# Stage A of a hybrid attention and MoE step: a round's work on ScalarE and VectorE reordered, the weight copy cut in two, the second adaLN half moved

## The chip, the cores and the metric

The kernel runs on one core of a Trainium2 chip. The metric is the device time of one execution in microseconds. A core has TensorE (matmul), VectorE, ScalarE, GpSimd and SyncE (which here only issues DMAs); each runs its own instruction stream in order, and they meet at semaphores. In rows of the profile they are PE (and PEld for the load of its weights), DVE, ACT, POOL and SP.

## The reference, cut to what matters

One layer for 256 prompt rows and 64 sample rows of width 1024, float32:

```python
h = RMSNorm(x) * (1 + scale1) + shift1          # scale, shift: adaLN, mod = silu(c) @ w_ada + b_ada
proj = h @ w_in                                 # A: q|k|v, B: q|k|v, gate_A, gate_B
# A: 8 heads, two 64-wide softmax maps per head (q, k RMS-normed, rotary), values 128 wide
s = einsum(q, k); p = softmax(where(mask, s, NEG_INF))
a = p[0] - lam * p[1]
o = rmsnorm(a @ v, subln_g) * (1 - lam_init)
# B: stick-breaking attention, 16 heads of 64
mix = sigmoid(gate_A) * (A @ w_oa) + sigmoid(gate_B) * (B @ w_ob)
x += gate1 * (mix @ w_out)
x += gate2 * HierMoE(RMSNorm(x) * (1 + scale2) + shift2)   # top-2 of 8 experts in 1 of 4 groups
```

The change is in stage A: the projection of the A columns and the differential attention. All its quantities are still computed.

## The kernel before

The stages follow each other: norm and first adaLN columns, stage A (to about 241 us), the gate and output product of A, stage B, its mix, the output product, the router and the experts.

Stage A is a software pipeline over the 8 heads. The function `a_iteration(h, ...)` exists once on each of the engines TensorE, ScalarE and VectorE; it is called for h = 0 to 10 (h = 4 to 7 from a hardware loop), and each call is what the text calls a round. Round h works on four heads at once:

- it projects head h (`P_on`, h up to 7): first the 64 sample rows as one float32 product (`proj_sample`, 32 matmuls), then tile 0 and tile 1 of 128 prompt rows each (`proj_tile`), each of 8 steps of 3 matmuls, since a float32 product is made of high and low parts: hi x hi, hi x lo, lo x hi (`mm3`, L546 to L548);
- it norms, rotates and transposes q and k of head h-1 (`qk_on`, h = 1 to 8) and makes the scores and exponentials of its prompt part (the first part of its maps);
- it makes the sample part of the maps of head h-2 and the transposes of the finished map (`s1_on`, h = 2 to 9);
- it makes the product with the values (PV), the norm and the transposes of the output of head h-3 (`o_on`, h = 3 to 10), and with it two chunks of the later adaLN columns (`ada_chunk(h, 0)` and `ada_chunk(h, 1)`, 32 small matmuls each, into bank 1, columns 384 to 511).

TensorE's order in a steady round: sample projection; PV; ada_chunk 0; scores of the sample part; tile 0; transposes of `o_n` (L688); four transposes of q and k (L696); ada_chunk 1; a wait for `a_olo`, that is for VectorE's `oT_lo`, which reads the bank that the next transposes write; four more transposes (L701); tile 1; transposes of the map (L716); scores of the prompt part.

ScalarE's order: `sq` (squares of q and k, L1093); root for q and k (`ss_ln`, `rs`: L1036, L1038); the whole high part of the next head's weights `w_hi` (`split`, L1069); copy of the sample's projection to `stage` (`stage_out(2, 0)`, L1111); `osq` (squares of PV, L1121) and root `o_rs`; exponentials of the sample part (L1127); copy of tile 0 (L1115); `oT_hi` (L1134); copy of half of the q/k transposes (L1138); copy of tile 1; `late_rows` (the adaLN results, L1143); copy of the map's transposes `aT` (L1146); exponentials of the prompt part (L1151).

VectorE's order: `ss` (sums of `sq`, L1433); q and k times `rs` ("scale", L1437); `o_ss` (sums of `osq`, L1441); `o_n` (L1445); maximum of the sample part (L1449) and its negation `a_nmx` (L1451); `combine` (L1417 to L1425: the two maps into `amap`); `oT_lo` (L1457); copy of the other half of the q/k transposes (L1461); the low part of the weights `w_lo` (L1365); rest of `aT` (L1466); maxima and combine of the prompt part.

GpSimd multiplies q and k by their gains (L1754), rotates them (L1764 to L1768, the last one gives `a_roped`) and keeps the values (L1773). SyncE issues, in a round and in this order: the next weights (`a_weights`, after `split_done` and the sample's projection), four stores of `stage` (`a_store`, after `a_roped`), the caches, and the two adaLN chunks (`load_late`, each after a chunk was used, by `late_used`). A copy to `stage[j]` waits until the stores of two heads before have landed (`a_stored[j]`). Weights and staging have double buffers (`raw`, `w_hi`, `w_lo`, `stage`). The next sample projection waits for `split_done`, which VectorE's `w_lo` gives.

Of the kernel before, what the change touches and what calls it, by code (L numbers as in the profile page):

```python
# [7 lines left out]
P = 128  # L8
D = 1024
# [70 lines left out]
def build(nc, t_in, t_out):  # L80
    g = t_in
    ctx = ExitStack()
    with ctx:
        def sem(name):
            return ctx.enter_context(nc.semaphore(name))
# [65 lines left out]
        sq = take("sq", [P, TILES, 256])  # L151
        osq = place("osq", [P, TILES, P], F32, cursor[0] - 4 * TILES * 256)
        ss = take("ss", [P, 12])
# [10 lines left out]
        a_sum = take("a_sum", [P, 2, 3])  # L164
        a_rec = take("a_rec", [P, 2, 3])
        o_ss = take("o_ss", [P, 3])
        o_ln = take("o_ln", [P, 3])
        o_rs = take("o_rs", [P, 3])
        o_n = take("o_n", [P, TILES, P])
        h_sample = take("h_sample", [P, KD, DEC])  # L170
        a_end = cursor[0]
# [5 lines left out]
        assert ada_at[4] + 8 * D + 2 * D <= raw_at  # L177
        late_rows = place("late_rows", [P, D], F32, hT_at - 4 * KD * PADDED)
        ada_late = [take(f"ada_late{n}", [P, KD, ADA_COLS]) for n in range(2)]
# [106 lines left out]
        h_mod = sem("h_mod"); h_hi = sem("h_hi"); h_ready = sem("h_ready")  # L286
        split_hi = sem("split_hi"); split_done = sem("split_done");

# [51 lines left out]
        def f32(ap):  # L340
            return ap.bitcast(F32)
# [198 lines left out]
        def _(pe):  # L540
# [108 lines left out]
            def a_iteration(h, j, P_on, qk_on, s1_on, o_on, cache_value):  # L649
# [34 lines left out]
                if o_on:  # L684
                    l = h - 3
                    pe.wait_ge(a_on, l + 1)
                    for t in range(TILES):
                        last = nc.tensor.transpose(ps[:, 4, t * P:(t + 1) * P], o_n[:, t, :], ident)  # L688
                    last.then_inc(a_oT, 1)
                if qk_on:  # L690
                    m = h - 1
                    pe.wait_ge(a_roped, m + 1)
                    pe.wait_ge(a_cache[jq], cache_value)
                    st = stage[jq]
                    for n, src in enumerate((st[:, 0, 0:P], st[:, 1, 0:P], st[:, 2, 0:P], st[:, 0, P:2 * P])):
                        nc.tensor.transpose(ps[:, 3, n * P:(n + 1) * P], src, ident)  # L696
                    if o_on:
                        ada_chunk(h, 1)
                        pe.wait_ge(a_olo, h - 2)
                    for n, src in enumerate((st[:, 1, P:2 * P], a_kc[jq][:, 0, :], a_kc[jq][:, 1, :], st[:, 2, P:2 * P])):  # L700
                        last = nc.tensor.transpose(ps[:, 4, n * P:(n + 1) * P], src, ident)  # L701
                    last.then_inc(a_qkT, 1)
                elif o_on:
                    ada_chunk(h, 1)
                if P_on:
# [32 lines left out]
            for n in range(8):  # L738
                last = nc.tensor.transpose(ps[:, 5 + n // 4, (n % 4) * P:(n % 4 + 1) * P], late_rows[:, n * P:(n + 1) * P], ident)
            last.then_inc(col_T, 1)  # L740
# [281 lines left out]
        def _(act):  # L1022
# [38 lines left out]
            def split(j, loaded, used, width=UNIT):  # L1061
# [7 lines left out]
                A(w_hi[j][:, :, 0:width], raw[j][:, :, 0:width], ACT.Copy).then_inc(split_hi, 1)  # L1069

            split(0, None, None)
            act.wait_ge(ada_used, KD)
# [3 lines left out]
            for t in range(2):  # L1076
                for half in range(2):
                    ks = slice(4 * half, 4 * half + 4)
                    act.wait_ge(h_mod, 2 * t + half + 2)
                    A(hT_hi[:, ks, t * P:(t + 1) * P], h_full[:, ks, t * P:(t + 1) * P], ACT.Copy).then_inc(h_hi, 1)  # L1080
            A(hT_hi[:, :, SEQ:TOK], h_sample[:], ACT.Copy).then_inc(h_hi, 1)
            act.wait_ge(lam_dve, 1)
            A(lam_exp[:], lam_sum[:], ACT.Exp).then_inc(lam_act, 1)

            def a_iteration(h, j, P_on, qk_on, s1_on, o_on, loaded, store_value):
                jq = 1 - j
                if qk_on:
                    act.wait_ge(a_staged, 3 * h)
                    if isinstance(h, int) and h == 1:
                        act.wait_ge(setup_done, 2)  # L1090
                    else:
                        act.wait_ge(a_ss, h - 1)
                    A(sq[:], stage[jq][:, :, 0:256], ACT.Square).then_inc(a_sq, 1)  # L1093
                    act.wait_ge(a_ss, h)
                    if not (isinstance(h, int) and h == 1):
                        act.wait_ge(a_scaled, h - 1)
                    root(rs[:], ss_ln[:], ss[:], 64, a_rs)
                if loaded is not None:
                    split(jq, loaded, None if isinstance(h, int) and h == 0 else (a_proj, 3 * h),
                          MIX_COLS if isinstance(h, int) and h >= 7 else UNIT)  # L1100

                def stage_out(t, n):
# [11 lines left out]
                    else:  # L1114
                        A(stage[j][:, t, :], ps[:, t, 0:UNIT], ACT.Copy).then_inc(a_staged, 1)  # L1115

                if P_on:
                    stage_out(2, 0)
                if o_on:
                    act.wait_ge(a_pv, h - 2)  # L1120
                    A(osq[:], ps[:, 7, 0:PADDED].rearrange("p (t c) -> p t c", t=TILES), ACT.Square).then_inc(a_osq, 1)  # L1121
                    act.wait_ge(a_oss, h - 2)
                    root(o_rs[:], o_ln[:], o_ss[:], P, a_ors)
# [8 lines left out]
                if o_on:  # L1132
                    act.wait_ge(a_oT, h - 2)
                    A(oT_hi[:, bass.ds(h - 3, 1), :].rearrange("p a n -> p (a n)"), ps[:, 4, 0:TOK], ACT.Copy,  # L1134
                      scale=subln[:, 0:1]).then_inc(a_ohi, 1)
                if qk_on:
                    act.wait_ge(a_qkT, h)
                    A(qkT[:, 0:512], ps[:, 3, :], ACT.Copy).then_inc(a_qkT_act, 1)  # L1138
                if P_on:
                    stage_out(1, 2)  # L1140
                if o_on:
                    act.wait_ge(late_used, 2 * h - 4)
                    A(late_rows[:, bass.ds((h - 3) * P, P)], ps[:, ADA_BANK, 384:512], ACT.Copy).then_inc(late_out, 1)  # L1143
                if s1_on:
# [165 lines left out]
        def _(dve):  # L1310
# [89 lines left out]
            dve.wait_ge(h_hi, 5)  # L1400
            V.tensor_tensor(hT_lo[:, :, SEQ:TOK], h_sample[:], f32(hT_hi[:, :, SEQ:TOK]), ALU.subtract).then_inc(h_ready, 1)
            dve.wait_ge(rows_in, 144)
# [26 lines left out]
            def a_iteration(h, j, qk_on, s1_on, o_on, split_on):  # L1429
                jq = 1 - j  # L1430
                if qk_on:
                    dve.wait_ge(a_sq, h)
                    V.tensor_reduce(ss[:].rearrange("p (t n) -> p t n", t=TILES),  # L1433
                                    sq[:].rearrange("p t (n c) -> p t n c", n=4), AX, ALU.add).then_inc(a_ss, 1)
                    dve.wait_ge(a_rs, h)
                    st = stage[jq][:, :, 0:256].rearrange("p t (n c) -> p t n c", n=4)
                    V.tensor_tensor(st, st, rs[:].rearrange("p (t n) -> p t n", t=TILES).unsqueeze(3).broadcast_to([P, TILES, 4, 64]),  # L1437
                                    ALU.mult).then_inc(a_scaled, 1)
                if o_on:
                    dve.wait_ge(a_osq, h - 2)  # L1440
                    V.tensor_reduce(o_ss[:], osq[:], AX, ALU.add).then_inc(a_oss, 1)  # L1441
                    dve.wait_ge(a_ors, h - 2)
# [19 lines left out]
                if split_on:  # L1462
                    split(h + 1, jq, MIX_COLS if isinstance(h, int) and h >= 7 else UNIT)
                if s1_on:
# [456 lines left out]
```

## Time and profile before

| | |
|---|---|
| median of 3 runs | 859.41 us (856.08 to 861.2) |
| profiled execution, its own time | 860.19 us |
| its span in the profile | 858.5 us |
| TensorE matmul busy | 714.1 us (83%) |
| VectorE busy | 347.3 us (40%) |
| ScalarE busy | 270.1 us (31%) |
| GpSimd busy | 102.1 us (12%) |
| mean granted clock of TensorE | 0.933 of full speed |

The span counts from the first to the last instruction. Matmuls are pipelined: their ends are modelled and overlap the next one's start, so a busy TensorE isn't one at its peak. A number in square brackets behind a row is the idle time of that engine before it, with the instruction that ended it. An engine that isn't the bottleneck may be idle without costing anything.

### The profile page before, as it was taken

The numbers are of one execution on the slowest core, as the hardware profiler recorded it, in microseconds if no ns is written. First come the engines' busy times: TensorE is split into PE (matmuls) and PEld (weight loads), VectorE is DVE, ScalarE is ACT, GpSimd is POOL, SyncE is SP. The second block draws the span as 40 slices with busy tenths as digits, with TensorE's granted clock in tenths as the row PEclk, the third lists the DMA queues.
The fourth block names the chain that finished last, engine by engine and source line by source line (L and its number), as shares of the span: only waits on it lengthen the run. The fifth ranks groups of instructions, "written<-read, shape, count | busy, mean of one in ns | idle before, by whom it ended". The sixth has DMA issues, their size and how long they took to land.

```text
span 858.5 us, 13770 instructions
## 1 busy us (share of the span) xinstructions
PE 714.1 (83%) x5329; PEld 586.5 (68%) x5329; DVE 347.3 (40%) x539; ACT 270.1 (31%) x490; POOL 102.1 (12%) x161
## 2 busy tenths in 40 slices
PE   0798888899799799999988999736998888788770
PEld 0487777788599798999987999634654554545440
DVE  0656555556534334333442356541233113213225
ACT  1454455454335254444544442300111011101100
POOL 2011111111000001010010000010011100100014
PEclk9899999999899899999999999857999999999985
DMA  9966466555643666452315443499899999999805
GB/s 323 321 167 197 132 181 176 174 172 175 195 152 111 175 172 226 118 139 63 110 44 163 147 133 113 165 424 416 324 418 417 418 418 418 417 417 419 332 17 183
DMA packets 131176, 199.17 MB, mean 232 GB/s; under 512 B 11688, under 2 KB 113464, under 8 KB 117816
## 3 DMA queue, kind: packets, MB, share of 16 engines
q1 hardware_dynamic: 123032, 185.63, 61.1%
q0 software_dynamic: 6208, 11.02, 3.6%
q10 hardware_dynamic: 1888, 1.86, 0.7%
q8 instruction: 32, 0.52, 0.2%
q14 instruction: 16, 0.13, 0.0%
HBM read 193.47 MB, written 16.55 MB: 245 GB/s over the span
## 4 chain that ended last, share of the span: by engine, by line
PE 52%; issue 22%; ACT 9%; DVE 8%; DVEq 3%; POOL 2%; POOLq 2%; ACTq 1%; DMA 0%
PE ps L551 29%; PE ps L546 6%; PE ps L548 6%; PE ps L547 6%; ACT w_hi L1069 3%; DVE w_lo L1365 2%; ACT probs L1151 1%; PE ps L948 1%; PE ps L952 1%; PE ps L984 1%; ACT probs L1127 1%; DVE amap L1425 1%; DVEq L1450 1%; PE ps L716 1%; DVE ss L1433 1%
## 5 line engine op out<-in xcount | busy, mean ns | idle before, releaser
L551 PE MATMUL ps<-e_w,xgT 128*64 128x256 f32 x1024 | 130.2, 418 | 31.9 <-issue 30.7
L551 PEld LDWEIGHTS ps<-e_w,xgT 128*64 128x64 f32 x1024 | 91.8, 151 | 66.1 <-issue 37.4
L1365 DVE TENSOR_TENSOR w_lo<-raw,w_hi 128x2048 fp32r<-128x2048 f32 (+1 forms) x36 | 100.5, 2793 | 86.2 <-ACT w_hi L1069 86.2
L546 PE MATMUL ps<-hT_hi,w_hi 128*128 128x320 f32 x320 | 102.7, 321 | 5.5 <-DVE w_lo L1365 5.2
L548 PE MATMUL ps<-hT_hi,w_lo 128*128 128x320 f32 x320 | 100.0, 312 | 0.0
L547 PE MATMUL ps<-hT_lo,w_hi 128*128 128x320 f32 x320 | 99.9, 312 | 0.0
L1069 ACT ACTIVATE w_hi<-raw 128x2048 fp32r<-128x2048 f32 (+1 forms) x36 | 83.2, 2310 | 28.5 <-PE ps L548 28.5
L1686 DVE TENSOR_SCALAR h_s<-h_e 128x256 f32<-128x256 f32 x16 | 4.7, 294 | 162.3 <-ACT h_e L1282 162.3
L546 PEld LDWEIGHTS ps<-hT_hi,w_hi 128*128 128x128 f32 x320 | 61.2, 191 | 7.9 <-DVE w_lo L1365 5.5
L547 PEld LDWEIGHTS ps<-hT_lo,w_hi 128*128 128x128 f32 x320 | 61.2, 191 | 0.0
L548 PEld LDWEIGHTS ps<-hT_hi,w_lo 128*128 128x128 f32 x320 | 61.1, 191 | 0.0
L551 PE MATMUL ps<-e_w,hidT 128*64 128x512 f32 x256 | 58.4, 598 | 0.6 <-ACT hidT L1288 0.6
L1282 ACT ACTIVATE h_e<-ps 128x256 f32<-128x256 f32 x16 | 6.1, 384 | 153.7 <-PE ps L551 153.7
L546 PE MATMUL ps<-w_hi,hT_hi 128*128 128x384 f32 x128 | 44.3, 346 | 0.0
L548 PE MATMUL ps<-w_hi,hT_lo 128*128 128x384 f32 x128 | 42.9, 335 | 0.0
L547 PE MATMUL ps<-w_lo,hT_hi 128*128 128x384 f32 x128 | 42.8, 335 | 0.0
L1860 POOL DMA_INDIRECT expert_rows<-y_sb,idx x16 | 16.2, 1012 | 215.0 <-DVE y_sb L1699 200.8
L546 PE MATMUL ps<-oT_hi,w_hi 128*128 128x320 f32 x128 | 40.4, 315 | 1.1 <-DVE oT_lo L1524 1.1
L547 PE MATMUL ps<-oT_lo,w_hi 128*128 128x320 f32 x128 | 40.3, 315 | 0.0
L548 PE MATMUL ps<-oT_hi,w_lo 128*128 128x320 f32 x128 | 40.2, 314 | 0.0
L551 PEld LDWEIGHTS ps<-e_w,hidT 128*64 128x64 f32 x256 | 17.5, 136 | 29.6 <-issue 27.8
L551 PE MATMUL ps<-ada_late,c_cols 128*32 128x128 f32 x512 | 33.1, 285 | 0.0
(258 smaller groups left out, 1225.6 us busy)
## 6 DMA issues: line engine op xcount, KB each, us to landing
e_w<-in_w SPq DMA_DIRECT2D x96, 1024.0 KB, 18.3
raw<-in_w_in SPq DMA_DIRECT2D x45, 512.0 KB
ada_late<-in_w_ada SPq DMA_DIRECT2D x16, 1024.0 KB, 5.0
ada_first<-in_w_ada SPq DMA_DIRECT2D x8, 1024.0 KB, 21.3
raw<-in_w_in SPq DMA_DIRECT2D x8, 1024.0 KB
raw<-in_w_oa SPq DMA_DIRECT2D x4, 1024.0 KB
raw<-in_w_ob SPq DMA_DIRECT2D x4, 1024.0 KB
raw<-in_w_out SPq DMA_DIRECT2D x4, 1024.0 KB
```

The costliest lines, as they stand in the source:

```text
L546: nc.tensor.matmul(out, lhs_hi, rhs_hi, start=first, stop=False, skip_group_check=True)
L547: nc.tensor.matmul(out, lhs_hi, rhs_lo, start=False, stop=False, skip_group_check=True)
L548: return nc.tensor.matmul(out, lhs_lo, rhs_hi, start=False, stop=last, skip_group_check=True)
L551: return nc.tensor.matmul(out, lhs, rhs, start=first, stop=last, skip_group_check=True)
L716: last = nc.tensor.transpose(ps[:, b, c * P:(c + 1) * P], amap[:, n * P:(n + 1) * P], ident)
L948: last = nc.tensor.transpose(ps[:, 0, k * P:(k + 1) * P], xg[p % RING][:, k:D:KD], ident)
L952: last = nc.tensor.transpose(ps[:, 1, (k - 4) * P:(k - 3) * P], xg[p % RING][:, k:D:KD], ident)
L984: last = nc.tensor.transpose(ps[:, 4, m * P:(m + 1) * P], hid[j][:, m:FE:2], ident)
L1069: A(w_hi[j][:, :, 0:width], raw[j][:, :, 0:width], ACT.Copy).then_inc(split_hi, 1)
L1127: last = A(probs[mp][:, 384:704], ps[:, 5 + mp, 0:320], ACT.Exp, bias=a_nmx[:, mp, 2:3], accum_out=a_sum[:, mp, 2:3])
L1365: V.tensor_tensor(w_lo[j][:, :, 0:width], raw[j][:, :, 0:width], f32(w_hi[j][:, :, 0:width]), ALU.subtract).then_inc(split_done, 1)
L1860: G.indirect_dma_start(y_dram, bass.IndirectOffsetOnAxis(ap=idx[:, 1, p:p + 1], axis=0), y_sb[j][:], None, bounds_check=2 * TOK, oob_is_er ...
```

## The change

On ScalarE a round now runs: sq; copy of the sample's projection; osq; root for q and k; root `o_rs`; exponentials; copy of tile 0; oT_hi; the first half of the weights' high part (the first 4 of 8 row blocks); its half of the q/k copy; the second half; the rest as before. On VectorE `o_ss` stands before the scaling of q and k, and the low part is made in two halves, each after its half of the high part. On TensorE `ada_chunk(h, 1)` stands directly behind the transposes of `o_n`, before those of q and k. `osq` gets memory of its own in place of the tail of `sq`; `h_sample` and `late_rows` move into the columns of `xnT` that are free.

```diff
-        osq = place("osq", [P, TILES, P], F32, cursor[0] - 4 * TILES * 256)
+        osq = take("osq", [P, TILES, P])
-        h_sample = take("h_sample", [P, KD, DEC])
-        late_rows = place("late_rows", [P, D], F32, hT_at - 4 * KD * PADDED)
+        late_rows, h_sample = xnT[:, :, 0:P], xnT[:, :, TOK:PADDED]
@@ TensorE
                     last.then_inc(a_oT, 1)
+                    ada_chunk(h, 1)
                 if qk_on:
...
                     if o_on:
-                        ada_chunk(h, 1)
                         pe.wait_ge(a_olo, h - 2)
...
-                elif o_on:
-                    ada_chunk(h, 1)
@@ ScalarE
+            def split_first(j, loaded, used, width):
+                act.wait_ge(raw_loaded[j], loaded - 48 * (1 - j))
+                if used is not None:
+                    act.wait_ge(*used)
+                A(w_hi[j][:, 0:KD // 2, 0:width], raw[j][:, 0:KD // 2, 0:width], ACT.Copy).then_inc(split_half, 1)
+            def split_second(j, width):
+                A(w_hi[j][:, KD // 2:KD, 0:width], raw[j][:, KD // 2:KD, 0:width], ACT.Copy).then_inc(split_hi, 1)
...
                 if qk_on:
                     act.wait_ge(a_staged, 3 * h)
...
                     A(sq[:], stage[jq][:, :, 0:256], ACT.Square).then_inc(a_sq, 1)
-                    act.wait_ge(a_ss, h)
-                    if not (isinstance(h, int) and h == 1):
-                        act.wait_ge(a_scaled, h - 1)
-                    root(rs[:], ss_ln[:], ss[:], 64, a_rs)
-                if loaded is not None:
-                    split(jq, loaded, None if isinstance(h, int) and h == 0 else (a_proj, 3 * h),
-                          MIX_COLS if isinstance(h, int) and h >= 7 else UNIT)
                 if P_on:
                     stage_out(2, 0)
                 if o_on:
                     act.wait_ge(a_pv, h - 2)
+                    if not (isinstance(h, int) and h == 3):
+                        act.wait_ge(a_oss, h - 3)
                     A(osq[:], ps[:, 7, 0:PADDED].rearrange("p (t c) -> p t c", t=TILES), ACT.Square).then_inc(a_osq, 1)
+                if qk_on:
+                    act.wait_ge(a_ss, h)
+                    if not (isinstance(h, int) and h == 1):
+                        act.wait_ge(a_scaled, h - 1)
+                    root(rs[:], ss_ln[:], ss[:], 64, a_rs)
+                if o_on:
                     act.wait_ge(a_oss, h - 2)
                     root(o_rs[:], o_ln[:], o_ss[:], P, a_ors)
...
+                width = MIX_COLS if isinstance(h, int) and h >= 7 else UNIT
+                if loaded is not None:
+                    split_first(jq, loaded, None if isinstance(h, int) and h == 0 else (a_proj, 3 * h), width)
                 if qk_on:
                     act.wait_ge(a_qkT, h)
                     A(qkT[:, 0:512], ps[:, 3, :], ACT.Copy).then_inc(a_qkT_act, 1)
+                if loaded is not None:
+                    split_second(jq, width)
@@ VectorE
+                if o_on:
+                    dve.wait_ge(a_osq, h - 2)
+                    V.tensor_reduce(o_ss[:], osq[:], AX, ALU.add).then_inc(a_oss, 1)
+                if qk_on:
                     dve.wait_ge(a_rs, h)
...
                 if o_on:
-                    dve.wait_ge(a_osq, h - 2)
-                    V.tensor_reduce(o_ss[:], osq[:], AX, ALU.add).then_inc(a_oss, 1)
                     dve.wait_ge(a_ors, h - 2)
...
                 if split_on:
-                    split(h + 1, jq, MIX_COLS if isinstance(h, int) and h >= 7 else UNIT)
+                    width = MIX_COLS if isinstance(h, int) and h >= 7 else UNIT
+                    for n, (signal, value) in enumerate(((split_half, h + 1), (split_hi, h + 2))):
+                        ks = slice(n * KD // 2, (n + 1) * KD // 2)
+                        dve.wait_ge(signal, value)
+                        last = V.tensor_tensor(w_lo[jq][:, ks, 0:width], raw[jq][:, ks, 0:width], f32(w_hi[jq][:, ks, 0:width]),
+                                               ALU.subtract)
+                    last.then_inc(split_done, 1)
```

## Rows read from the trace of the kernel before

**Rows 1.** Stretches: us, busy us (instructions) of each engine, clock, DMA share, GB/s

```profile
108.60:200.40 91.80, 81.93 (x743) 71.54 (x741) 51.93 (x96) 43.98 (x108) 16.68 (x24) 1.00 0.61 184
320.00:410.00 90.00, 88.87 (x708) 82.30 (x707) 33.50 (x41) 41.18 (x58) 10.10 (x30) 1.00 0.48 141
```

**Rows 2.** Waits of TensorE from 90 to 205: total us, times, longest

```profile
PE ps L701 <- DVE oT_lo L1457: 6.3, 5, 1.5
PE ps L688 <- DVE o_n L1445: 5.8, 5, 1.2
```

**Rows 3.** Timeline of TensorE, round 5: start, us, instruction [idle before]

```profile
131.49 2.82 PE L551 MATMUL ps<-raw,h_sample 128*64 128x192 f32 x32
...
135.77 1.94 PE L551 MATMUL ps<-ada_late,c_cols 128*32 128x128 f32 x32
...
142.48 0.34 PE L548 MATMUL ps<-w_hi,hT_lo 128*128 128x384 f32 x1
143.97 0.55 PE L688 MATMUL ps<-cst,o_n 128*128 128x128 f32 x3 [1.15 <-DVE o_n L1445]
...
144.88 1.94 PE L551 MATMUL ps<-ada_late,c_cols 128*32 128x128 f32 x32
148.33 0.33 PE L701 MATMUL ps<-cst,stage 128*128 128x128 f32 x1 [1.51 <-DVE oT_lo L1457]
...
154.60 2.82 PE L551 MATMUL ps<-raw,h_sample 128*64 128x192 f32 x32
```

**Rows 4.** Timeline of ScalarE, round 5

```profile
134.94 0.85 ACT L1093 ACTIVATE sq<-stage 128x768 f32<-128x768 f32 x1
137.75 0.30 ACT L1036 ACTIVATE ss_ln<-ss,eps 128x12 f32<-128x12 f32 x1 [1.96 <-DVE ss L1433]
...
138.30 2.78 ACT L1069 ACTIVATE w_hi<-raw 128x3072 fp32r<-128x3072 f32 x1
140.97 0.65 ACT L1111 ACTIVATE stage<-ps 64x192 f32<-64x192 f32 x2
```

**Rows 5.** Timeline of VectorE, round 5

```profile
136.77 0.95 DVE L1433 TENSOR_REDUCE ss<-sq 128x12 f32<-128x768 f32 x1
138.37 0.96 DVE L1437 TENSOR_TENSOR stage<-stage,rs 128x768 f32<-128x768 f32 x1 [0.65 <-ACT rs L1038]
...
143.83 0.82 DVE L1449 TENSOR_REDUCE a_mx<-ps 128x2 f32<-128x640 f32 x1
...
147.73 0.55 DVE L1457 SCALAR_TENSOR_TENSOR oT_lo<-ps,subln,oT_hi 128x320 f32 x1
```

**Rows 6.** Groups by form, 60 to 345 us: busy us, mean ns | idle before

```profile
L1365 DVE TENSOR_TENSOR w_lo<-raw,w_hi 128x3072 fp32r<-128x3072 f32 x11 | 36.9, 3352 | 18.1 <-ACT w_hi L1069 18.1
...
L1365 DVE TENSOR_TENSOR w_lo<-raw,w_hi 128x2048 fp32r<-128x2048 f32 x7 | 16.0, 2291 | 24.4 <-ACT w_hi L1069 24.4
```

**Rows 7.** Timelines of round 1: TensorE, ScalarE, GpSimd

```profile
54.18 2.82 PE L551 MATMUL ps<-raw,h_sample 128*64 128x192 f32 x32 [1.35 <-DVE w_lo L1365]
...
61.21 0.60 PE L696 MATMUL ps<-cst,stage 128*128 128x128 f32 x4
...
55.25 0.31 ACT L1036 ACTIVATE ss_ln<-ss,eps 128x12 f32<-128x12 f32 x1 [1.02 <-DVE ss L1433]
...
60.35 0.60 POOL L1768 TENSOR_TENSOR stage<-rope_x,rope_y 128x192 f32<-128x192 f32 x1
```

**Rows 8.** Timeline of TensorE, round 8

```profile
215.41 0.33 PE L701 MATMUL ps<-cst,stage 128*128 128x128 f32 x1 [0.53 <-DVE oT_lo L1457]
```

**Rows 9.** Timelines of round 2: VectorE and GpSimd

```profile
75.88 1.13 DVE L1451 TENSOR_SCALAR a_nmx<-a_mx 128x2 f32<-128x2 f32 x1
...
75.15 1.84 POOL L1754 TENSOR_TENSOR stage<-stage,gqk 128x768 f32<-128x768 f32 x1 [13.75 <-DVE stage L1437]
```

**Rows 10.** Timeline of SyncE's issues; landing times of DMAs of `stage`, 147 to 170

```profile
154.95 0.54 SPq L390 DMA_DIRECT2D out_a_v_sample<-stage  x1
...
DMA to landing us min/median/max: 3.5/4.0/5.5
```

More of the change, by code:

```diff
@@ L286, in build @@
         h_mod = sem("h_mod"); h_hi = sem("h_hi"); h_ready = sem("h_ready")
-        split_hi = sem("split_hi"); split_done = sem("split_done");
+        split_half = sem("split_half"); split_hi = sem("split_hi"); split_done = sem("split_done");
         a_cache = [sem(f"a_cache{j}") for j in range(2)]
@@ L738, in _ @@
             for n in range(8):
-                last = nc.tensor.transpose(ps[:, 5 + n // 4, (n % 4) * P:(n % 4 + 1) * P], late_rows[:, n * P:(n + 1) * P], ident)
+                last = nc.tensor.transpose(ps[:, 5 + n // 4, (n % 4) * P:(n % 4 + 1) * P], late_rows[:, n, :], ident)
             last.then_inc(col_T, 1)
@@ L1080, in _ @@
                     A(hT_hi[:, ks, t * P:(t + 1) * P], h_full[:, ks, t * P:(t + 1) * P], ACT.Copy).then_inc(h_hi, 1)
-            A(hT_hi[:, :, SEQ:TOK], h_sample[:], ACT.Copy).then_inc(h_hi, 1)
+            A(hT_hi[:, :, SEQ:TOK], h_sample, ACT.Copy).then_inc(h_hi, 1)
             act.wait_ge(lam_dve, 1)
@@ L1086, in a_iteration @@
                 jq = 1 - j
[L1087 to L1093, printed above, removed]
-                    act.wait_ge(a_ss, h)
-                    if not (isinstance(h, int) and h == 1):
-                        act.wait_ge(a_scaled, h - 1)
-                    root(rs[:], ss_ln[:], ss[:], 64, a_rs)
-                if loaded is not None:
-                    split(jq, loaded, None if isinstance(h, int) and h == 0 else (a_proj, 3 * h),
-                          MIX_COLS if isinstance(h, int) and h >= 7 else UNIT)
                 def stage_out(t, n):
@@ L1115, in stage_out @@
                         A(stage[j][:, t, :], ps[:, t, 0:UNIT], ACT.Copy).then_inc(a_staged, 1)
+                if qk_on:
+                    act.wait_ge(a_staged, 3 * h)
+                    if isinstance(h, int) and h == 1:
+                        act.wait_ge(setup_done, 2)
+                    else:
+                        act.wait_ge(a_ss, h - 1)
+                    A(sq[:], stage[jq][:, :, 0:256], ACT.Square).then_inc(a_sq, 1)
                 if P_on:
@@ L1142, in a_iteration @@
                     act.wait_ge(late_used, 2 * h - 4)
-                    A(late_rows[:, bass.ds((h - 3) * P, P)], ps[:, ADA_BANK, 384:512], ACT.Copy).then_inc(late_out, 1)
+                    A(late_rows[:, bass.ds(h - 3, 1), :].rearrange("p a n -> p (a n)"), ps[:, ADA_BANK, 384:512], ACT.Copy).then_inc(late_out, 1)
                 if s1_on:
@@ L1400, in _ @@
             dve.wait_ge(h_hi, 5)
-            V.tensor_tensor(hT_lo[:, :, SEQ:TOK], h_sample[:], f32(hT_hi[:, :, SEQ:TOK]), ALU.subtract).then_inc(h_ready, 1)
+            V.tensor_tensor(hT_lo[:, :, SEQ:TOK], h_sample, f32(hT_hi[:, :, SEQ:TOK]), ALU.subtract).then_inc(h_ready, 1)
             dve.wait_ge(rows_in, 144)
@@ L1434, in a_iteration @@
                                     sq[:].rearrange("p t (n c) -> p t n c", n=4), AX, ALU.add).then_inc(a_ss, 1)
+                if o_on:
+                    dve.wait_ge(a_osq, h - 2)
+                    V.tensor_reduce(o_ss[:], osq[:], AX, ALU.add).then_inc(a_oss, 1)
+                if qk_on:
                     dve.wait_ge(a_rs, h)
```

## The prediction

> **What bounds the kernel now.** I began with the page's busy shares: TensorE has by far the most work. Then the busy time by stretches, to see the stage that the diff touches [rows 1]: in the steady rounds of stage A TensorE is busy 81.93 of 91.80 us at a granted clock of 1.00, VectorE and ScalarE hardly half, the DMA engines 0.61. Then the waits of TensorE in that stretch, which ask what it lacked [rows 2]: only two things hold it there, 5 times each, once in each of the rounds h = 3 to 7: the transposes of o_n (L688) wait for VectorE's o_n, 5.8 us in all, and the second half of the q/k transposes (L701) waits for VectorE's oT_lo, 6.3 us. So TensorE sets the pace and is held by a chain through ScalarE and VectorE that is late by 1.2 us at two places of a round. Last the timelines of one round on each engine, to see why that chain is late.
>
> I give times in a round as t from the start of its sample projection. Round 5 runs from 131.49 to 154.60, 23.11 us, the first adaLN chunk follows PV at t = 4.3, and tile 0's last matmul starts at 142.48, t = 11.0 [rows 3]. The 24 matmuls of a tile go 0.17 apart, so TensorE could go on at 11.2; the matmul is drawn 0.34 long, so a stop costs the idle time shown (1.15 here) and 0.16 of lost overlap, 0.07 behind the short chunk matmuls. Without its two waits this round is 23.11 - 1.15 - 1.51 - 0.23 = 20.2 us [rows 3]. ScalarE's order is what makes o_n late [rows 4]: sq at 3.45 (to 4.3), the root for q/k at 6.26 when VectorE's ss is there, then the whole weight copy w_hi, 2.78 us, and only at 9.48 the copy of the sample's projection, which TensorE had finished at 2.75, and behind it osq, though PV was ready at 4.3. osq, o_ss, o_n, the map's maximum, exponentials, combine and oT_lo all hang behind this one copy.
>
> **What the change does to a steady round.** ScalarE: sq to 4.3, the sample's copy (0.65) to 4.95, osq (0.5) to 5.45. VectorE is no help earlier: it ends the combine of the former map at 5.3 and ss at 5.28 + 0.94 = 6.2 [rows 5]; o_ss follows to 6.75. The root of ss is not delayed (it waits for ss at 6.26 as before), scale starts at 6.88 as before and ends at 7.84; o_rs is there at 7.4, so o_n runs 7.8 to 8.4. Before, o_n was ready at 12.5. TensorE wants it at 11.2: the first wait is gone, with 2.8 us to spare.
> The map's maximum starts at 8.26 instead of 12.34 (143.83); from its start to oT_lo's end it took 147.73 + 0.55 - 143.83 = 4.45 us [rows 5]. That gives 12.7, with oT_hi ready before it (the transposes of o_n end at 11.7, ScalarE's copy at 12.3). Now the second adaLN half (ada_chunk(h, 1)) stands straight behind the o_n transposes: TensorE comes to L701 at 11.2 + 0.9 for seven transposes (143.97 to 144.88) + 1.9 for the chunk = 14.0 [rows 3]. oT_lo is there 1.3 us before. GpSimd's rope ends 5.7 us after the root starts (60.95 - 55.25 in round 1, rows below), so at 12.0, and is wanted at 13.5. So both waits go. Their worth: 5.8 + 6.3 idle + 5 x (0.16 + 0.07) of lost overlap = 13.3 us over the five rounds.
> The weight halves: VectorE's subtraction costs 2.29 us for 2048 and 3.35 for 3072 elements [rows 6], 1.04 ns each and 0.17 fixed, so two halves cost 0.17 more, ScalarE's likewise about 0.18. In a steady round they lie under the projection of tile 1, 4.2 us: ScalarE's first half 12.3 to 13.8, q/k copy 14.7 to 15.3, second half to 16.7; VectorE's 15.3 to 18.7, the aT copy is wanted at 19.5. Cost nothing; if the cover were gone, 0.2 a round. What is late next: nothing on TensorE, if these sums hold. The move of ada_chunk is 32 matmuls from behind L696 to before it, same work; its data is asked for 18 us ahead. It moves SP's raw and store issues too: they follow late_used, now at t = 13.5.
> Buffers (osq on its own, h_sample and late_rows inside xnT): same instructions, I take zero; nothing of them is on a path with less than 1 us of slack.
>
> **The ends of the loop.** Round 0: the weight copy no longer stands before the copies of the projection, but behind tile 0's, 49.0 to 51.8; VectorE's halves end at 53.8 against 54.13: gain 0.3.
> Round 1 loses. There the root for q/k ran at 55.25, at once, and the rope ended at 60.95, just before TensorE wanted it at 61.21 [rows 7]. In the new order the root is queued behind the copy of the sample's projection, and that is only ready when TensorE ends it: 54.18 + 2.82 - 0.3 = 56.7, and copied by 57.4. The root moves from 55.25 to 57.4, 2.15 later, and scale and rope with it: rope's end 60.95 + 2.15 = 63.1. L696 goes from 61.2 to 63.1: loss 1.9 net of the 0.3. In round 2 the sample is done long before sq, so its root is not moved; its own wait for the rope stays, and nothing there gives the 1.9 back.
> Round 8 (no projection; the gate is TensorE's filler): the wait of 0.53 before L701 [rows 8] and 0.07 overlap go; but there the split stands before the aT copy that TensorE waits for next, and its halves cost 0.1 more: gain 0.5. Rounds 9 and 10 run the same chain as before.
> **Sum:** 13.3 - 1.9 + 0.5 = 11.9 us. All later stages start from it and their loads are gated by the same semaphores, so it goes through to the end. The profiled execution took 860.19 us (span 858.5); that gives 848.3. It lies 0.8 above the median of 859.41, from which the forecast is **847.5**.
>
> **Two contentions.** First, GpSimd. In round 2 VectorE's tiny negation L1451 took 1.13 us instead of 0.17 and ended at 77.01, when GpSimd's L1754, running since 75.15, ended at 76.99 [rows 9]. In the steady rounds of before the rope ran while VectorE was idle. Now L1754 runs from 7.9 to 9.8, over the negation at 9.15: that ends at 9.8, 0.5 later, and the four short rope instructions (to 12) lie over the combine. Bounds: nothing more, or one of them waited for at each of combine's three steps, together 0.9. oT_lo at 13.2 to 14.1 against 14.0; I take 13.3, as in round 2 the combine was hardly longer: no loss. The Trainium skill, "SBUF — State Buffer", section "Who interferes with whom", states that a VectorE instruction in a 2-port mode or with two SBUF inputs and a GpSimd one exclude each other for a whole instruction; the trace agrees with it at L1451, and by it the high bound is the likelier one, 13.3 + 0.7, at the edge.
> Second, the stores. The last store of a round is issued at 154.95, and the stores there take 3.5 to 5.5 us to land [rows 10]; with 3.5 that is 158.45, 13.6 after the second chunk's start at 144.88. Now that start is t = 11.6, so landing is at 25.2, t = 5.0 of the next 20.2-us round, while the sample's copy, which overwrites that stage buffer, could start at 4.3. Before, it started at 9.5 and the landing was hidden. ScalarE will wait 0.7 us here, with osq and both roots behind it; that much goes under ss. Both contentions together put oT_lo at 13.4 to 14.3: low bound no loss, high bound 0.3 a round, 1.5 us.
>
> **Rivals.** (a) The forecast, waits gone and nothing in their place: chance 0.62, own range 845 to 850. It could be some us better: a stretch at half clock follows the waits of rounds 9 and 10, and may fall otherwise.
> (b) oT_lo stays the last to come: the port exclusion at every step, and stores 2 us later than in the trace. Then 1.0 to 1.5 of a round's 2.65 come back: 5 x 1.25 = 6.3, time 853.8. For it: the burst of loads and stores fills the DMA engines already. Against: only sums of bad bounds reach it. It is a slower wait at the same L701. Chance 0.23.
> (c) No change that can be measured (within 0.5%, 4.3 us, about what a measurement of this kernel can tell): the round is held by something the trace hides, the stores or instruction fetch, and round 1's loss and perhaps a second one at the seams stand against what is left; 857. Chance 0.10.
> (d) Slower: TensorE without pauses is granted less clock in rounds 3 to 7. A fall from 1.00 to 0.89 would eat the gain (101 us x (1 / 0.89 - 1) = 12), below it the kernel is slower; at half clock for 20 us it gives 857.5, for 50 us 872. Against it: from 320 to 410 us TensorE was busy 88.87 of 90 us at a clock of 1.00 [rows 1]. Chance 0.05 for over 0.5% slower, with the stores' mechanism in it: ScalarE's wait for a_stored would have to end 6 us later than I work out before it eats all of a round's gain, since a longer round gives the stores time.
> Range: 844 to 855 leaves out (c), (d) and the tail of (b). Faster by over 0.5% are (a) and (b): 0.85; same 0.10; slower 0.05.
>
> **What will show it.** In the profile after: waits of TensorE on o_n (L688) and on oT_lo (L701) gone in rounds 3 to 7, rounds 20.2 us apart; in round 1 a new wait of TensorE at L696 for the rope of some 2.2 us; ScalarE waiting up to 1 us for a store before the sample's copy; the negation L1451 0.6 us long, under GpSimd's L1754; copy halves of 1.5 and 1.75 us. Rounds over 20.6, or a wait at L701 that stays over 0.5, say (b). The forecast is wrong if the granted clock in these rounds is under 1.00 or the later stages lose what stage A wins.

## The result and the profile after

The changed kernel takes 848.92 us (median of 8 runs, 846.17 to 853.51) against 858.87 us for the kernel before (8 runs). The ratio is 0.9889 with a 95% interval of 0.9863 to 0.9915, so 1.1% faster. Forecast were 847.5 us and a gain of 11.9; the ratio says 9.5, and so do the spans of the two profiled executions, 858.5 and 849.0 us.

First, what TensorE still waits for from 50 to 245 us: the four largest rows (us in all, times, longest). The changed file's lines are a little shifted: L550 is the old L551, L687 the old L688, L700 the old L701, L713 the old L716.

```profile
PE ps L696 <- POOL stage L1789: 5.1, 2, 3.2
PE ps L687 <- DVE o_n L1460: 3.1, 2, 2.6
PE ps L550 <- DVE w_lo L1482: 1.3, 1, 1.3
PE ps L713 <- DVE qkT L1476: 0.9, 1, 0.9
...
```

The two rows of [rows 2], 12.1 us, are gone from the steady rounds. What is left on o_n belongs to rounds 9 and 10; the row on top is the rope, in rounds 1 and 2. Round 5 on TensorE, to be laid beside [rows 3]:

```profile
131.90 2.82 PE L550 MATMUL ps<-raw,xnT 128*64 128x192 f32 x32
...
136.19 1.94 PE L550 MATMUL ps<-ada_late,c_cols 128*32 128x128 f32 x32
...
143.07 0.49 PE L687 MATMUL ps<-cst,o_n 128*128 128x128 f32 x3
143.49 1.94 PE L550 MATMUL ps<-ada_late,c_cols 128*32 128x128 f32 x32
145.37 0.65 PE L696 MATMUL ps<-cst,stage 128*128 128x128 f32 x4
146.03 0.33 PE L700 MATMUL ps<-cst,stage 128*128 128x128 f32 x1
...
152.31 2.82 PE L550 MATMUL ps<-raw,xnT 128*64 128x192 f32 x32
```

No bracket stands behind any of these rows: the o_n transposes follow tile 0 at once, at t = 11.2, and the round takes 20.41 us instead of 23.11. Only between L696 and L700 there are 0.66 us where rounds 3, 6 and 7 have 0.49 (round 4 has 0.56), so something still holds L700 by 0.17.

What holds it is on the other engines. ScalarE and VectorE in the same round:

```profile
135.36 0.85 ACT L1116 ACTIVATE sq<-stage 128x768 f32<-128x768 f32 x1
137.88 0.66 ACT L1104 ACTIVATE stage<-ps 64x192 f32<-64x192 f32 x2 [1.67 <-issue]
138.57 0.49 ACT L1123 ACTIVATE osq<-ps 128x384 f32<-128x384 f32 x1
```

```profile
139.09 0.55 DVE L1450 TENSOR_REDUCE o_ss<-osq 128x3 f32<-128x384 f32 x1 [0.96 <-ACT osq L1123]
139.57 0.96 DVE L1454 TENSOR_TENSOR stage<-stage,rs 128x768 f32<-128x768 f32 x1
140.44 0.55 DVE L1460 TENSOR_TENSOR o_n<-ps,o_rs 128x384 f32<-128x384 f32 x1
140.91 0.82 DVE L1464 TENSOR_REDUCE a_mx<-ps 128x2 f32<-128x640 f32 x1
141.80 0.68 DVE L1466 TENSOR_SCALAR a_nmx<-a_mx 128x2 f32<-128x2 f32 x1
...
144.05 0.76 DVE L1435 TENSOR_SCALAR amap<-probs,a_rec 128x320 f32<-128x320 f32 x1
...
145.44 0.54 DVE L1472 SCALAR_TENSOR_TENSOR oT_lo<-ps,subln,oT_hi 128x320 f32 x1
```

The copy of the sample's projection is at t = 6.0 and not at 4.3: ScalarE stood 1.67 us for something that the row doesn't name. VectorE's negation, 0.17 us alone, takes 0.68, and oT_lo ends at 145.98, t = 14.08, when L700 was due at 145.86. Against 16.8 before (147.73 + 0.55, [rows 5]) that is 2.7 us earlier, and just enough.

GpSimd in these microseconds:

```profile
140.61 1.85 POOL L1775 TENSOR_TENSOR stage<-stage,gqk 128x768 f32<-128x768 f32 x1 [15.83 <-DVE stage L1454]
...
144.03 0.59 POOL L1789 TENSOR_TENSOR stage<-rope_x,rope_y 128x192 f32<-128x192 f32 x1
```

L1775 ends at 142.46, the negation at 142.48. In the profile of before the two met only in round 2 [rows 9]; now they meet in every steady round.

Where the 9.5 us of the profiles come from is seen by cutting each TensorE timeline at the start of the sample projections, at PV of round 8 and at the transposes of late_rows (starts from the timelines, differences in us; the later columns are of the experiments below):

```
                     before   after    e1      e2      e3      e4      e5      e7      e8      e9
start of round 0      39.78   40.42   39.87   40.51   40.28   39.62   39.81   39.64   39.50   40.13
round 0               14.40   15.56   14.35   14.26   15.57   15.57   14.36   15.33   15.57   14.38
round 1               13.04   15.22   13.02   18.50   15.20   13.82   16.79   13.03   13.03   13.03
round 2               18.70   20.26   18.69   20.20   18.68   20.01   18.68   19.95   16.89   16.90
rounds 3 to 7        114.43  101.18  101.28  108.39  101.37  102.15  100.83  101.79  101.53  100.83
rounds 8 to 10        40.90   38.52   37.53   38.86   38.79   37.59   38.87   37.64   37.74   37.53
rest of the span     617.25  617.84  618.36  620.78  617.11  620.74  617.26  620.62  620.84  620.30
span                  858.5   849.0   843.1   861.5   847.0   849.5   846.6   848.0   845.1   843.1
```

(e1 to e9 are the runs below by the first part of their names.) Rounds 3 to 7 gave 13.25 us; forecast were 13.3. The other rows are small and of both signs, and a good part of them is the clock. The granted clock of a stretch stands in the column before the DMA share; in the records it is either 1.00 or 0.50 of full speed (half clock), and a stretch shows the mean. Here are a stretch of the changed kernel's execution at the start of stage A, one in round 2, the steady rounds, and one in round 9:

```profile
36.00:46.00 10.00, 6.69 (x37) 5.08 (x38) 7.96 (x29) 2.86 (x5) 0.00 (x0) 0.51 0.75 164
...
83.00:88.00 5.00, 4.84 (x22) 4.84 (x23) 4.51 (x5) 2.87 (x3) 0.65 (x2) 0.66 0.26 69
...
91.46:192.64 101.18, 101.17 (x927) 89.61 (x925) 69.19 (x125) 55.34 (x140) 21.41 (x30) 1.00 0.64 195
...
217.60:224.40 6.80, 5.94 (x41) 4.41 (x42) 3.14 (x9) 2.42 (x7) 0.00 (x0) 0.53 0.32 96
```

Before, the same stretches showed 0.83, 1.00 (79 to 84), and 0.57 over 11.80 us (226.2 to 238) where the changed kernel has 0.53 over 6.80. In the steady rounds TensorE is now busy 101.17 of 101.18 us at a clock of 1.00: the rival that a TensorE without pauses is granted less clock is answered.

### The profile page after: what moved, and what is told of

Its sections match the earlier page's. It is cut to its first block, busy times and chain, and to the rows that moved or that the text cites. A ratio compares the mean times of both kernels' runs of the same rounds, so it can differ in the third digit from the quotient of the medians.

```text
span 849.0 us, 13795 instructions
## 1 busy us (share of the span) xinstructions
PE 714.0 (84%) x5329; PEld 585.2 (69%) x5329; DVE 349.2 (41%) x548; ACT 271.0 (32%) x499; POOL 102.9 (12%) x161
## 4 chain that ended last, share of the span: by engine, by line
PE 63%; issue 20%; ACT 6%; DVE 4%; POOL 2%; POOLq 2%; ACTq 1%; DVEq 1%; DMA 0%
PE ps L550 35%; PE ps L545 8%; PE ps L547 7%; PE ps L546 7%; ACT w_hi L1066 3%; DVE w_lo L1378 1%; PE ps L945 1%; PE ps L949 1%; PE ps L981 1%; PE ps L713 1%; ACT sig_r L1183 1%; DVEq L1587 1%; ACT z_na L1228 1%; PE ps L696 0%; POOLq L1777 0%
## 5 line engine op out<-in xcount | busy, mean ns | idle before, releaser
L550 PE MATMUL ps<-e_w,xgT 128*64 128x256 f32 x1024 | 129.7, 417 | 32.6 <-issue 31.3
L550 PEld LDWEIGHTS ps<-e_w,xgT 128*64 128x64 f32 x1024 | 91.2, 151 | 66.8 <-issue 40.2
L1378 DVE TENSOR_TENSOR w_lo<-raw,w_hi 128x2048 fp32r<-128x2048 f32 (+1 forms) x27 | 71.5, 2647 | 83.9 <-ACT w_hi L1066 83.9
L1066 ACT ACTIVATE w_hi<-raw 128x2048 fp32r<-128x2048 f32 (+1 forms) x27 | 59.1, 2190 | 28.3 <-PE ps L547 28.3
L550 PE MATMUL ps<-e_w,hidT 128*64 128x512 f32 x256 | 58.4, 598 | 0.6 <-ACT hidT L1301 0.6
L550 PEld LDWEIGHTS ps<-e_w,hidT 128*64 128x64 f32 x256 | 17.5, 136 | 29.6 <-issue 27.8
L550 PE MATMUL ps<-ada_late,c_cols 128*32 128x128 f32 x512 | 32.7, 283 | 0.0
```

The costliest lines, as they stand in the source:

```text
L550: return nc.tensor.matmul(out, lhs, rhs, start=first, stop=last, skip_group_check=True)
L1378: V.tensor_tensor(w_lo[j][:, :, 0:width], raw[j][:, :, 0:width], f32(w_hi[j][:, :, 0:width]), ALU.subtract).then_inc(split_done, 1)
```

## The experiments

Times are medians; ratios are to the kernel before, run on the same chip; the changed kernel was not timed again beside the experiments, so two ratios are compared and not two medians. Executions of one kernel spread over 5 us and more, so what a run tells of one or two us is read from its profile, by the table above.

**Round 1's root first (e1_root1).** In round 1 alone the root goes ahead of the sample's copy again.

```diff
                     A(sq[:], stage[jq][:, :, 0:256], ACT.Square).then_inc(a_sq, 1)
+                if qk_on and (isinstance(h, int) and h == 1):
+                    act.wait_ge(a_ss, h)
...
+                    root(rs[:], ss_ln[:], ss[:], 64, a_rs)
                 if P_on:
                     stage_out(2, 0)
...
-                if qk_on:
+                if qk_on and not (isinstance(h, int) and h == 1):
                     act.wait_ge(a_ss, h)
```

> The changed kernel, but in round 1 alone ScalarE makes the root of q and k ahead of the copy of the sample's projection, as before the change. My account: the rope of round 1 is ready for TensorE, the wait of 1.96 us at L696 in round 1 goes, and with the overlap the kernel is 2.2 us faster than the changed one, about 846.7. If the half clock from 84 to 88 us in round 2 followed from the two pauses (1.96 and 3.16 us) in a row, it goes as well: 1.6 us more, about 845. Rival 1: the pause of round 1 is only moved into round 2, where TensorE waits for the rope anyway: the wait there grows from 3.16 to 5 us and the time stays at 849. Rival 2: the half clock is chance: round 2 at 18.7 or 20.3 us with no relation to round 1.

Measured: 845.22 us, ratio 0.9828 (0.9800 to 0.9856). Round 1 took 13.02 us instead of 15.22, and of the rope's two waits one is left:

```profile
PE ps L696 <- POOL stage L1794: 3.1, 1, 3.1
```

Round 2 did not grow, so rival 1 is out: the loss of 2.2 us in round 1 was real and stood alone. Round 2 ran at full clock here. Whether that followed from round 1 only the next runs tell.

**The second adaLN chunk put back (e2_chunk_back).**

```diff
                     last.then_inc(a_oT, 1)
-                    ada_chunk(h, 1)
...
                     if o_on:
+                        ada_chunk(h, 1)
                         pe.wait_ge(a_olo, h - 2)
...
```

> The changed kernel with the second adaLN chunk back behind the first four transposes of q and k. L701 is reached at the same time as now (t = 14.0), but L696 already at 11.6, where the rope ends at 12.7 in the changed kernel. My account: a wait of 1.1 us and 0.16 of overlap at L696 in each of rounds 3 to 8, 6 to 7.5 us slower than the changed kernel, about 856, and most of the gain is gone. Rival: the chunk's place is cosmetic, as the seven transposes and the chunk stand between tile 0 and L701 in either order: 849.

Measured: 856.74 us, ratio 0.9972 (0.9947 to 0.9996). Most of the gain is gone. TensorE's waits in rounds 3 to 7 (93 to 202 us), and round 4:

```profile
PE ps L695 <- POOL stage L1791: 6.3, 5, 3.1
```

```profile
125.45 0.55 PE L687 MATMUL ps<-cst,o_n 128*128 128x128 f32 x3
129.12 0.65 PE L695 MATMUL ps<-cst,stage 128*128 128x128 f32 x4 [3.12 <-POOL stage L1791]
129.70 1.94 PE L550 MATMUL ps<-ada_late,c_cols 128*32 128x128 f32 x32
131.57 0.33 PE L700 MATMUL ps<-cst,stage 128*128 128x128 f32 x1
```

The five rounds take 108.39 us, 7.2 more than in the changed kernel. The seven transposes and the chunk fill the same time in either order, but without the chunk before it L695 comes to a rope that isn't ready. So the move of the chunk, which looks like tidying, is needed for more than half of the steady gain: without it 6.0 of the 13.25 us are left. The sum came as I said (6 to 7.5 us), but not by the 1.1 us a round that I gave for it: the five waits were 0.33, 3.12, 1.66, 0.78 and 0.41 us. ScalarE waited 3.8 us for the landing of a store in round 4, 2.2 in round 5 and 1.3 in round 6, and the root behind it moved the rope; that the total fits is in part luck. This also means that the 7.2 us are the chunk's worth in the changed kernel's order, where the root stands behind a copy that waits for the stores; its worth in the old order wasn't measured.

The profiled execution, 863.32 us, is the slowest of 12. Its round 1 took 18.50 us at a mean clock of 0.82, 3.3 more than the changed kernel's, though the edit touches nothing before round 3.

**The weight copies whole (e3_whole).**

```diff
-                    split_first(jq, loaded, None if isinstance(h, int) and h == 0 else (a_proj, 3 * h), width)
+                    split(jq, loaded, None if isinstance(h, int) and h == 0 else (a_proj, 3 * h), width)
...
-                if loaded is not None:
-                    split_second(jq, width)
```

(and on VectorE one subtraction in place of two)

> The changed kernel with the weight copies whole (high part where the first half stands, low part one instruction). My account: in the steady rounds both lie under tile 1's projection, and nothing changes (ScalarE's q/k copy comes 0.4 us later, TensorE wants it 3 us later). Only in round 0 VectorE can't start on the first half, so that the next sample projection waits 1.1 us longer (2.4 instead of 1.3); round 8 wins 0.1. Together 1.0 us slower than the changed kernel, 850. Rival: the halves carry the gain, as ScalarE's q/k copy behind a whole copy holds the map's transposes: 0.4 us or more in each of rounds 3 to 7, 852 or more.

Measured: 847.16 us, ratio 0.9870 (0.9835 to 0.9904), not to be told from the changed kernel. In the profile rounds 3 to 7 take 101.37 against 101.18 us: the halves don't carry the gain. In round 0 the next projection waits longer for the weights, as said, 2.5 against 1.3:

```profile
PE ps L696 <- POOL stage L1781: 5.1, 2, 3.2
...
PE ps L550 <- DVE w_lo L1376: 2.5, 1, 2.5
```

This run also has both rope waits, 5.1 us in all, as the changed kernel, and its round 2 took 18.68 us at full clock. So the two pauses alone do not bring the half clock in round 2.

**Only the two moves (e4_move_only).** The weight copy is whole and behind oT_hi, the chunk is moved; root, sample's copy, scale and o_ss stand in the order of before.

```diff
                     A(sq[:], stage[jq][:, :, 0:256], ACT.Square).then_inc(a_sq, 1)
+                if qk_on:
+                    act.wait_ge(a_ss, h)
...
+                    root(rs[:], ss_ln[:], ss[:], 64, a_rs)
                 if P_on:
                     stage_out(2, 0)
...
-                if o_on:
-                    dve.wait_ge(a_osq, h - 2)
-                    V.tensor_reduce(o_ss[:], osq[:], AX, ALU.add).then_inc(a_oss, 1)
-                if qk_on:
                     dve.wait_ge(a_rs, h)
...
```

> Of the change only two moves: the whole weight copy stands behind oT_hi on ScalarE, and the second adaLN chunk behind the transposes of o_n. The root of q and k stands ahead of the copy of the sample's projection and VectorE scales ahead of o_ss, as before; osq keeps its own memory. My account: this has the steady gain (ScalarE is 0.6 us later at the sample's copy, but it waited 1.7 us for the stores there anyway; oT_lo at t = 14.1 against 14.0, so 0.0 to 0.2 us a round at L701), no loss in round 1 (2.2 faster than the changed kernel) and 1.1 lost in round 0 because the copy is whole: 1.1 us faster than the changed kernel, 848, or 846 if the half clock of round 2 goes too. Rival: the order of delivery of the osq and o_ss work is needed, o_n or oT_lo come late again by 0.6 us or more a round: 852.

Measured: 850.1 us, ratio 0.9897 (0.9869 to 0.9926). I expected 848 or less, and half of that account was wrong. Right is the steady part: 102.15 us for rounds 3 to 7, 12.3 of the 13.25 us without any of the finer reordering, the rest a last wait at L700, once 0.56:

```profile
144.21 0.33 PE L700 MATMUL ps<-cst,stage 128*128 128x128 f32 x1 [0.56 <-DVE oT_lo L1473]
```

Missed was round 1: the whole copy, now behind tile 0, ends at 65.6, VectorE starts on it after its q/k copy, and the next projection waits:

```profile
69.01 2.82 PE L550 MATMUL ps<-raw,xnT 128*64 128x192 f32 x32 [0.73 <-DVE w_lo L1381]
```

And round 2 again took 20.01 us with a stretch at half clock, although the pause of round 1 was only 0.73 us. The rest of its span was 620.7 us where the changed kernel had 617.8; that part of the program is the same, so 3 us of this single execution are no effect of the edit. They go with the clock: behind stage A the ten profiled executions fall into two groups, 617.1 to 618.4 us at a mean granted clock of 0.92 (before, after, e1, e3, e5) and 620.3 to 620.8 us at 0.91 (e2, e4, e7, e8, e9).

**The old order with halves (e7_old_order_halves).** As the last, with the halves of the changed kernel.

> As the run with only the two moves (old order of root, sample's copy, scale and o_ss), but with the weight copies in halves. My account: round 0 back at 14.4 us instead of 15.6 and no wait for w_lo in round 1 (0.73), so 2 us faster than that run's profile; rounds 3 to 7 as there, 102.2 us together, 1 us more than with the new order. Against the changed kernel: round 1's 2.2 us won, 1 us of the steady rounds lost. Rival: the halves delay VectorE in the steady rounds and these take over 103 us.

Measured: 848.48 us, ratio 0.9850 (0.9801 to 0.9898); the span is 848.0, 1.5 less than that of the run before. Round 1 took 13.03 us, the wait for w_lo is gone; rounds 3 to 7 took 101.79, not above 103, 0.6 more than in the changed kernel. Round 0 did not show the gain, since it had half clock at its start (15.33). The halves are thus worth 1.2 us in round 0 (14.36 in e5 against 15.57 in e3, both with a clock of 0.88 to 0.89) and 0.8 in round 1 of this old order (in the new one nothing, 15.20 in e3 against 15.22). In the steady rounds they made 0.2 and 0.4 us in the two pairs, no more than two executions with the same steady rounds differ (101.18, 101.28 and 101.53 in the changed kernel, e1 and e8). The finer order of root, o_ss and scale is worth 0.6 to 0.8 us there, little above that, and costs 2.2 in round 1.

**The stores ahead of the weights (e5_stores_first).**

```diff
-                    a_weights(2 * i + j, j)
                     a_store(2 * i + j - 1, 1 - j)
+                    a_weights(2 * i + j, j)
```

> The changed kernel, but in the hardware loop of SyncE (rounds 3 to 6) the four stores of a head are issued ahead of the next weights, not behind them. My account: the stores land some 4 to 8 us earlier, ScalarE no longer waits before the copy of the sample's projection (1.67 us in round 5, named issue), osq and oT_lo come 0.5 to 0.8 us earlier, GpSimd's L1775 still covers the negation. TensorE gains only the 0.1 to 0.2 us by which oT_lo holds it in two of the rounds, so the time stays: 848.5 to 849. Rival: ScalarE's pause of 1.67 us is not the stores (the profile names no releaser), it stays as it is. Second rival: the weights now land late and hold the weight copy, slower by 1 us or more.

Measured: 848.96 us, ratio 0.9890 (0.9864 to 0.9917), the same as the changed kernel. From ScalarE's waits from 91 to 193 us, first in the changed kernel, then here:

```profile
...
ACT ss_ln L1033 <- DVE ss L1446: 2.1, 3, 0.9
ACT stage L1104 <- DMA out_a_v_sample<-stage: 2.1, 2, 1.5
ACT stage L1104 <- issue: 1.7, 1, 1.7
...
```

```profile
...
ACT qkT L1149 <- PE ps L700: 4.5, 5, 0.9
ACT ss_ln L1033 <- DVE ss L1446: 4.5, 5, 0.9
```

With the stores issued first all waits before the sample's copy are gone, the unnamed one too: it was a store. The negation stays at 0.67 us, as GpSimd still covers it:

```profile
139.08 0.67 DVE L1466 TENSOR_SCALAR a_nmx<-a_mx 128x2 f32<-128x2 f32 x1
```

Rounds 3 to 7 take 100.83 us, each 20.16 or 20.17: this is what TensorE's own work takes, and the changed kernel pays 0.35 us over it. The weights were not late: TensorE was busy 100.83 of the 100.83 us. Round 1 of this execution, which the edit doesn't touch, took 16.79 us at a mean clock of 0.90, 1.6 more than the changed kernel's at 1.00.

**Round 2 reordered too (e8_root1_round2).** To the kernel with round 1's root first: in round 2 tile 1 goes ahead of the q/k transposes.

```diff
+                early = isinstance(h, int) and h == 2
+                if P_on and early:
+                    proj_tile(h, j, 1, False)
                 if qk_on:
                     m = h - 1
...
-                if P_on:
+                if P_on and not early:
                     proj_tile(h, j, 1, isinstance(h, int) and h == 0)
...
```

> The kernel with round 1's root put first, and in round 2 tile 1 projected ahead of the q/k transposes, so that TensorE doesn't stand 3.1 us for the rope; there the weight copy's second half goes ahead of ScalarE's q/k copy, and VectorE's first half ahead of its own. My account: tile 1 takes 4.2 us and covers the rope's 3.1, but the map's transposes then wait 0.5 to 1 us for the q/k copies, round 2 takes 17.2 instead of 18.7 us: 1.5 us faster than with round 1's root alone. Rival: the next projection waits for w_lo and eats it all.

Measured: 844.4 us, ratio 0.9824 (0.9799 to 0.9850). Round 2 took 16.89 us instead of 18.69, 1.8 less; a wait of 1.4 us for the q/k copy took the place of 3.1 us for the rope:

```profile
PE ps L716 <- DVE qkT L1496: 1.4, 1, 1.4
```

By the medians it can't be told from the kernel without it. The other kernel's profiled execution is even the shorter one (843.1 against 845.1 us), by 1.2 us in round 0 (clock 0.88 against 0.81) and 2.5 behind stage A (0.92 against 0.91).

**All of it (e9_all).** With the stores first as well.

> The same with the stores ahead of the weights as well. My account: like the kernel without that, within 0.3 us in the profile's stage A; if oT_lo's last 0.1 us waits in rounds 4 and 5 go too, rounds 3 to 7 take 101.15 us. Rival: the weights land late, slower.

Measured: 840.68 us (840.05 to 844.92), ratio 0.9791 (0.9769 to 0.9813). Rounds 3 to 7 take 100.83 us, as in the run with the stores first, and 0.7 less than without it (101.53), where I had expected at most 0.3. This version beats both kernels: its interval lies below that of the changed kernel (0.9863 to 0.9915), by 1.0%, some 8 us, of which round 1 (2.2), round 2 (1.8 for the same clock) and the stores (0.35) explain 4.3 by the profiles. At least part of the rest goes with the clock: over the whole span the five executions of this version were granted 0.931 to 0.936 (the profiled one, with 0.931, is the slowest, 844.92 us), the eight of the changed kernel 0.929 to 0.931. How much of it that is, no run tells.

## Why the prediction was right

**The steady rounds.** Right in mechanism and size. The weight copy in front of the sample's projection was what made o_n and oT_lo late; with it moved both waits went, and rounds 3 to 7 gave 13.25 us for 13.3. e4_move_only shows that the move of the copy and that of the chunk give 12.3 of them together. No run undoes the copy's move alone, and the new places of osq, h_sample and late_rows are in every run; that the copy was the cause is read from the timelines (o_n ended at t = 12.4 before and at 9.1 after, oT_lo at 16.8 and 14.08), not from an experiment of its own.

**The chunk.** I gave its move no price ("same work") and wrote only that the rope is wanted at 13.5 and ready at 12.0. The run that undid it shows that 7.2 us, over half of the gain, hung on this line. The rope was ready at 12.7 (144.03 + 0.59), later than I had it, and still in time. The sum was right because the margin was there, but the text did not say what the margin was worth.

**The two contentions.** Both came as said. The negation was held by L1775 for 0.5 us; here the Trainium skill's rule ("SBUF — State Buffer", "Who interferes with whom") and the trace agree: a tiny VectorE instruction ended 0.02 us after the GpSimd instruction under which it had started. A 128x320 product (L1435) took 0.76 us for the 0.38 of an undisturbed round, beside GpSimd's L1789; it ended 0.19 us after that one, so this row shows that it was slowed, not that it stood until the other's end. The stores were worse than my 0.7 us: 1.67 us in round 5. oT_lo came at 14.08, in my range of 13.4 to 14.3, at a place due at 14.0. The cost was 0.35 us over five rounds (101.18 against 100.83 with the stores first). Rival (b), which needed 1.25 us in each round, had the right mechanisms at about a twentieth of its price (0.35 against 6.3 us).

**Round 1.** Right: forecast a wait of 2.2 us at L696 and 1.9 net, measured 1.96 of idle time and 2.2 in the length of the round. The 0.3 set against it, from VectorE's earlier end in round 0, did not come: in e1_root1 round 0 took 14.35 us against 14.40, since VectorE's two halves ran from 50.74 to 54.17 there, while I had them end at 53.8.

**Rounds 8 to 10, and the clock.** Forecast 0.5, measured 2.4. Round 8 alone, at a clock of 1.00 in both kernels, went from 19.08 to 18.33 us, 0.75 less; this is the order of work, and e1_root1 has the same 18.33. The change leaves the work of rounds 9 and 10 as it was: they took 21.82 us at a mean clock of 0.77 before, 20.19 at 0.83 after, and 19.20 at 1.00 in e1_root1. So 1.6 of the 2.4 us are clock. On the other side the execution lost 1.15 us in round 0 and 1.55 in round 2 to half clock, and 0.65 before them. Steady 13.25, round 8 0.75 and rounds 9 and 10 1.6, less round 0 1.15, round 1 2.2, round 2 1.55, the start 0.65 and the rest of the span 0.6, is 9.5. Of that the order of work is 13.25 + 0.75 - 2.2 = 11.8, where the forecast had 11.9. That it comes so close is in part luck: the 0.3 that round 0 didn't give and the 0.25 that round 8 gave above its forecast nearly cancel. The miss of 2.4 in the profiled pair is clock (0.65 + 1.15 + 1.55 - 1.6 = 1.75) and 0.6 behind stage A, at a mean clock of 0.92 in both, that no run assigns. Whether the medians' miss (9.5 by the ratio) has the same make-up was not measured, as only one execution of each kernel is profiled.

**Left open.** What decides the half clock of round 2. It came in four of the eight profiled kernels that have the wait of 3.1 us there (the changed one, e2, e4, e7) and not in the other four (the one before, e1, e3, e5); the size of round 1's pause doesn't decide it (e3 and the changed kernel both had the two pauses of round 1 and 2, 5.1 us in all, and only the latter half clock; e4 had 0.73 us before its round 2 and half clock). It isn't bound to round 2 either: in e2 and e5 round 1 had it (18.50 and 16.79 us against 15.2), with no edit there.

## What to carry to other kernels

When an engine with an in-order queue serves a pipeline, put the long work that nobody waits for (here a 2.8 us weight copy) behind the short work on which the bottleneck hangs; this move gave nearly all the gain together with a second one, filler work on TensorE (the chunk) put ahead of the result that comes latest, without which over half of it was lost; the finer ordering gave almost nothing. Order for the steady round and then walk the first rounds: an order of arrival that is right in round 5 had ScalarE wait in round 1 for a projection with a finished result of VectorE in hand. And when a copy becomes early, look for what its destination buffer still waits for: the stores, whose landing had been hidden, were the next wait at once, and issuing them ahead of the loads cost nothing that the profile or the time shows.

## What the runs showed of the hardware

Two rounds of the same instructions differed by 1.3 to 1.6 us with the granted clock, in the same place, from one kernel to another with no edit there (round 2: 18.68 to 18.70 us at 1.00, or 19.95 to 20.26 at 0.91 to 0.92), and once by 3.3 us (round 1 of the new order: 15.20 and 15.22 us at 1.00, 18.50 at 0.82). The 617 us behind stage A, where nothing but the places of buffers differs, differed by 3 us with a mean clock of 0.92 or 0.91. A difference of 2 us between single executions should be cut by stages before it is explained.

A VectorE instruction of two elements per partition took 0.66 to 0.68 us for 0.17 in all of rounds 3 to 8 of the changed kernel, since it started under a GpSimd instruction of some 1.85 us and ended with it.
